# MLP up projection computed transposed: weights stationary, both parts of the activations moving

## The chip, the cores and the metric

The kernel runs on one core of a Trainium2 chip. The metric is the device time of one execution in microseconds (us). The engines of the core run side by side, each through its own list of instructions, and wait for one another on semaphores: TensorE (PE, matrix products; PEld is its loading of the held operand), VectorE (DVE), ScalarE (ACT), GpSimd (POOL) and SyncE (SP), which issues the loads from memory.

## What is computed

One call runs three transformer layers on 256 tokens of width 1024, in float32: an attention layer, an mLSTM layer and a hybrid layer. Each ends in the same MLP, and that is what the change touches:

```python
D_MODEL, SEQ, D_FF = 1024, 256, 4096
def sqrelu_mlp(h, w1, w2):
    return jnp.square(jax.nn.relu(h @ w1)) @ w2
# first_block, for both layers:
h = h + mix
h = h + sqrelu_mlp(rmsnorm(h, mlp_norm[layer]), mlp_w1[layer], mlp_w2[layer])
# hybrid_layer:
x = x + jnp.square(jax.nn.relu(rms_norm(x, norm_mlp) @ w_up)) @ w_down
gate = jax.nn.sigmoid(rms_norm(x, norm_ple) @ w_ple_gate)
x = x + gate * (p_l @ w_ple)
```

## The kernel before

**Products in three parts.** TensorE multiplies in the type fp32r. To keep float32 accuracy every operand is split in two: `hi`, its rounding to fp32r (a copy by ScalarE), and `lo`, the rest (a subtraction by VectorE). A product is three matmuls into the same sum: hi by hi, hi by the weights' lo, lo by the weights' hi. The helper `product` issues them:

```python
pe.matmul(o, hi, whi, start=start, stop=False)              # L693
pe.matmul(o, hi, wlo, start=False, stop=False)              # L694
return pe.matmul(o, lo, whi, start=False, stop=stop)        # L695
```

The second argument of `pe.matmul` is the operand that is held (loaded into the array first, 128 x 128), the third is the one that moves through, here 512 columns. So 128 tokens' activations are held and 512 weight columns move; the result has tokens on its partitions. The profile and the lists of instructions name a matmul by `result<-moving,held`.

**Weights.** A unit is 1024 columns of weights on 128 partitions (512 KB). SyncE loads units in the order in which they are used into a ring of eight places `raw`; ScalarE makes `w_hi` of a unit (L1199), VectorE `w_lo` (L1633), each into a ring of eight. TensorE adds one to the semaphore `unit_used` with the last matmul on a unit, which frees the three places: SyncE loads the unit that is eight further into it. `lo_ready` tells TensorE that a unit is split.

**The MLP.** The 4096 hidden columns are done in eight steps of 512 (`steps`, `HALF`). Step i has two halves. `up` multiplies the normalised activations `a_hi`, `a_lo` (eight chunks of 128 rows, all 256 tokens) by four units of w1, into the two banks of `pair[0]`. ScalarE takes relu of a bank (L1263), VectorE multiplies relu by the positive part of the same bank (L1679), which gives `hid`, tokens on partitions. For the second product `hid` must be held with hidden columns on partitions, so `turn_hidden` (L822 to L827) turns it by eight TensorE transposes of 128 x 128 into `turn_ps`; ScalarE copies that to `h_hi` (L1270), VectorE subtracts to get `h_lo` (L1688). `down_step` multiplies them by four units of w2 and adds into `down`, that is `pair[1]` and `score`, four banks that stay open over all eight steps (opened by four matmuls with zeros, L865).

**Order.** On TensorE: `up_first`, zeros, `turn_hidden`, then a hardware loop of seven rounds (L867): `up` of step i, `down_step` of step i-1, `turn_hidden` of step i; then `down_last` of step 7 (L829), which goes through the result in two halves, so that the additions to `x` and the turns of the next stage start early. `up_first` finishes the first 128 tokens of its last two units before the others and says so by `up_half`. ScalarE and VectorE run their own loops (L1280, L1698): `step` empties the `up` result, splits four units, and splits the turned `hid`; `step_tail` splits four more.

**Entry.** The activations of an MLP come from `x` through transposes into the two banks of `turn_ps` (`x_turn`, helper line L721), two chunks at a time; ScalarE and VectorE split each into `a_hi`, `a_lo` (L1214, L1651). Chunks 0 to 3 are turned in the stage before, chunks 4 to 7 after the first unit of `up_first` (its slot 0), as soon as VectorE has added the second half of the stage before to `x` (L1730). In the third MLP slot 3 turns `p_sb` too (group `pT.0`, its parts `p_hi`, `p_lo` at L1212 and L1649), an input of the stage behind it. A group of turns waits until the group two before it, in the same bank, has been read.

## Time and profile before

| | |
|---|---|
| median of 3 runs | 1225.9 us (1225.36 to 1228.71) |
| profiled execution, span | 1225.7 us |
| TensorE matmul busy | 1189.9 us, 97% |
| TensorE loads busy | 973.1 us, 79% |
| VectorE busy | 717.6 us, 59% |
| ScalarE busy | 618.9 us, 50% |
| DMA queue of SyncE | 52% of 16 engines, 199.61 MB |

Busy time of TensorE says little by itself: a matmul's record is longer than the distance to the next one's start, since they overlap. What a piece of work costs is read from the starts in the timeline. The line in a row is that of a helper, so work is told apart by the names of its tiles. The granted clock (PEclk) is a share of TensorE's full 2.4 GHz: 1.00 is that, 0.50 is 1.2 GHz. A row of the timeline gives the start, the length, the engine, the line, and in square brackets the idle time before it with what ended it.

### The profile page before, as it was taken

What the parts mean: (1) busy time and instruction counts of PE and PEld (TensorE: products, weight loads), DVE (VectorE), ACT (ScalarE), POOL (GpSimd) and SP (SyncE); (2) the same over time, 40 slices, a digit from 0 to 9 for tenths busy, and PEclk for the clock granted to TensorE, in tenths of its full rate; (3) what the DMA queues carried; (4) which work ended last, traced back from release to release, by engine and by line L of the source; (5) the groups of instructions that cost most, each with busy time, mean ns of one, the idle gap of its engine ahead of it and who ended that gap; (6) DMA issues with size and microseconds to landing.
All of it is one profiled execution on the core that took longest, in us unless ns stands there. A gap on an engine that the chain in (4) does not pass through costs nothing.

```text
span 1225.7 us, 15495 instructions
## 1 busy us (share of the span) xinstructions
PE 1189.9 (97%) x5530; PEld 973.1 (79%) x5530; DVE 717.6 (59%) x955; ACT 618.9 (50%) x970; POOL 63.4 (5%) x77
## 2 busy tenths in 40 slices
PE   6899999999999999999998999998999999999997
PEld 5778788888788888888887887767888887888876
DVE  4678655455566664554577778543645565554554
ACT  5487534434447653444356455465654444443443
POOL 2001000000000100000021033000000000000000
PEclk9999999999989999999999999999999999999999
DMA  8743555555445455555556555432565655555542
GB/s 245 257 131 116 166 172 188 188 175 186 144 129 162 150 179 185 186 185 184 176 161 195 161 172 167 125 103 70 171 189 174 189 180 171 186 188 182 180 150 90
DMA packets 95121, 205.58 MB, mean 168 GB/s; under 512 B 7805, under 2 KB 10149, under 8 KB 95072
## 3 DMA queue, kind: packets, MB, share of 16 engines
q1 hardware_dynamic: 93216, 199.61, 52.0%
q0 software_dynamic: 1696, 5.26, 1.6%
q8 instruction: 29, 0.48, 0.2%
q14 instruction: 20, 0.16, 0.0%
q10 hardware_dynamic: 160, 0.07, 0.0%
HBM read 203.86 MB, written 2.63 MB: 168 GB/s over the span
## 4 chain that ended last, share of the span: by engine, by line
PE 90%; DMA 4%; ACT 2%; DVE 2%; issue 1%; SPq 0%; POOL 0%; ACTq 0%
PE pair L693 24%; PE pair L695 23%; PE pair L694 23%; PE score L694 4%; PE score L693 4%; PE score L695 4%; PE turn_ps L721 3%; PE turn_ps L826 2%; DMA raw<-in_attn_w_in 1%; DMA bias<-bias_replicas 1%; DMA bias_replicas<-bias_scratch 1%; PE score L1077 1%; DVE w_lo L1633 1%; DMA raw<-in_w_in 0%; ACT w_hi L1199 0%
## 5 line engine op out<-in xcount | busy, mean ns | idle before, releaser
L1633 DVE TENSOR_TENSOR w_lo<-raw,w_hi 128x1024 fp32r<-128x1024 f32 (+2 forms) x381 | 453.4, 1223 | 157.4 <-ACT w_hi L1199 142.6
L1199 ACT ACTIVATE w_hi<-raw 128x1024 fp32r<-128x1024 f32 (+2 forms) x381 | 383.7, 1049 | 137.9 <-DMA raw<-in_w_in 31.4
L693 PE MATMUL pair<-w_hi,a_hi 128*128 128x512 f32 (+3 forms) x944 | 380.4, 403 | 4.5 <-ACT lat_sb L1244 3.4
L695 PE MATMUL pair<-w_hi,a_lo 128*128 128x512 f32 (+3 forms) x944 | 369.4, 391 | 0.0
L694 PE MATMUL pair<-w_lo,a_hi 128*128 128x512 f32 (+3 forms) x944 | 368.5, 390 | 0.0
L693 PEld LDWEIGHTS pair<-w_hi,a_hi 128*128 128x128 f32 x944 | 181.3, 192 | 42.3 <-ACT lat_sb L1244 3.6
L695 PEld LDWEIGHTS pair<-w_hi,a_lo 128*128 128x128 f32 x944 | 181.0, 192 | 37.4
L694 PEld LDWEIGHTS pair<-w_lo,a_hi 128*128 128x128 f32 x944 | 181.7, 192 | 34.7 <-issue 1.2
L1679 DVE SCALAR_TENSOR_TENSOR hid<-pair,relu 128x512 f32<-128x512 f32 x48 | 31.2, 686 | 116.2 <-ACT relu L1263 116.2
L1263 ACT ACTIVATE relu<-pair 128x512 f32<-128x512 f32 x48 | 26.4, 595 | 142.8 <-PE pair L695 142.8
L1688 DVE TENSOR_TENSOR h_lo<-turn_ps,h_hi 128x512 fp32r<-128x512 f32 x48 | 30.9, 685 | 112.6 <-ACT h_hi L1270 112.6
L1270 ACT ACTIVATE h_hi<-turn_ps 128x512 fp32r<-128x512 f32 x48 | 26.0, 595 | 137.1 <-PE turn_ps L826 137.1
L693 PE MATMUL pair<-w_hi,h_hi 128*128 128x512 f32 x192 | 75.5, 393 | 3.2 <-DVE h_lo L1688 3.2
L694 PE MATMUL pair<-w_lo,h_hi 128*128 128x512 f32 x192 | 75.6, 394 | 0.0
L694 PE MATMUL score<-w_lo,h_hi 128*128 128x512 f32 x192 | 75.6, 394 | 0.0
L693 PE MATMUL score<-w_hi,h_hi 128*128 128x512 f32 x192 | 75.5, 393 | 0.0
L695 PE MATMUL score<-w_hi,h_lo 128*128 128x512 f32 x192 | 74.7, 389 | 0.0
L695 PE MATMUL pair<-w_hi,h_lo 128*128 128x512 f32 x192 | 74.6, 388 | 0.0
L693 PEld LDWEIGHTS pair<-w_hi,h_hi 128*128 128x128 f32 x192 | 36.0, 188 | 12.0 <-issue 3.8
L693 PEld LDWEIGHTS score<-w_hi,h_hi 128*128 128x128 f32 x192 | 36.0, 188 | 8.3
L695 PEld LDWEIGHTS score<-w_hi,h_lo 128*128 128x128 f32 x192 | 36.0, 188 | 8.1
L695 PEld LDWEIGHTS pair<-w_hi,h_lo 128*128 128x128 f32 x192 | 36.0, 188 | 8.0
(335 smaller groups left out, 1225.4 us busy)
## 6 DMA issues: line engine op xcount, KB each, us to landing
raw<-in_mlp_w SPq DMA_DIRECT2D x128, 512.0 KB, 3.4
raw<-in_w_in SPq DMA_DIRECT2D x64, 512.0 KB, 3.7
raw<-in_w_up SPq DMA_DIRECT2D x32, 512.0 KB, 3.6
raw<-in_w_down SPq DMA_DIRECT2D x32, 512.0 KB, 3.2
raw<-in_attn_w_in SPq DMA_DIRECT2D x24, 512.0 KB, 7.1
raw<-in_mlstm_w_in SPq DMA_DIRECT2D x24, 512.0 KB, 3.8
raw<-in_w_br SPq DMA_DIRECT2D x16, 512.0 KB, 3.7
raw<-in_attn_w_out SPq DMA_DIRECT2D x8, 512.0 KB, 3.7
```

The costliest lines, as they stand in the source:

```text
L693: pe.matmul(o, hi, whi, start=start, stop=False)
L694: pe.matmul(o, hi, wlo, start=False, stop=False)
L695: return pe.matmul(o, lo, whi, start=False, stop=stop)
L721: last = pe.transpose(bank[:, j * P:(j + 1) * P], src, ident)
L826: last = pe.transpose(turn_ps[:, tt, c * P:(c + 1) * P], hid[:, tt, c * P:(c + 1) * P], ident)
L1077: last = pe.matmul(o, lq_t[rows, h // 2, q], lk_t[rows, h // 2, k], start=False, stop=True)
L1199: act.activation(w_hi[:, k % RING, 0:n], raw[:, k % RING, 0:n], ACT.Copy).then_inc(hi_ready, 1)
L1263: act.activation(relu[:, tt, :], pair[0][:, tt, :], ACT.Relu).then_inc(up_relu, 1)
L1270: act.activation(h_hi[:, :, tt * P:(tt + 1) * P], turn_ps[:, tt, :].rearrange("p (c s) -> p c s", s=P), ACT.Copy)\
L1633: dve.tensor_tensor(w_lo[:, k % RING, 0:n], raw[:, k % RING, 0:n], w_hi[:, k % RING, 0:n], ALU.subtract).then_inc(lo_ready, 1)
L1679: dve.scalar_tensor_tensor(hid[:, tt, :], pair[0][:, tt, :], 0.0, relu[:, tt, :], ALU.max, ALU.mult).then_inc(hid_ready, 1)
L1688: dve.tensor_tensor(h_lo[:, :, rows], turn_ps[:, tt, :].rearrange("p (c s) -> p c s", s=P), h_hi[:, :, rows], ALU.subtract).then_inc(hid_l ...
```

## The change

`up` holds the weights now and moves the activations, so that its result has hidden columns on partitions: what `turn_hidden` made. `a_hi` and `a_lo` become the two halves of one tile `a_both`, 512 columns for a chunk. With 128 columns of `w_hi` held, one matmul moves both (512 columns: hi sum in the first 256 columns of a bank, the lo by w_hi product in the others); with `w_lo` held, a second moves `a_hi` (256 columns) onto the second half. The four groups of 128 hidden columns have a bank each, two in `pair[0]` and two in `turn_ps` (together `ups`). ScalarE copies the second halves out (`up_low`), VectorE adds them to the first (`up_sum`) and multiplies by the positive part (`hid`). `h_hi`, `h_lo` come from `hid` in SBUF. The last step writes them to tiles of its own, `e_hi`, `e_lo`. `turn_hidden`, `relu` and the semaphores `up_relu`, `hid_turned` are gone; `up_copied`, `up_summed` are new. `up_first` does `pair[0]` for all four units, then `turn_ps` for all four; all four units are freed in the second pass. The turn of `p_sb` moves to slot 1, its splits before `step`, and the second pass waits for them. In the loops ScalarE and VectorE split six units before `h_hi`, `h_lo` and two after.

```diff
-        a_hi = sb("a_hi", [DC, S], F32R)
-        a_lo = sb("a_lo", [DC, S], F32R)
+        a_both = sb("a_both", [DC, 2, S], F32R)
+        a_hi, a_lo = (a_both[:, :, i, :] for i in range(2))
...
+        ups = [pair[0], turn_ps]
...
-                def up(k, it):
+                def up_unit(k, u, pairs):
+                    slot = (k + u) % RING
+                    for j in range(2):
+                        c = 2 * u + j
+                        for i in pairs:
+                            for b in range(2):
+                                at_col = j * HALF + (2 * i + b) * P
+                                cols = slice(at_col, at_col + P)
+                                pe.matmul(ups[i][:, b, :], w_hi[:, slot, cols], a_both[:, c, :, :],
+                                          start=c == 0, stop=False)
+                                last = pe.matmul(ups[i][:, b, S:], w_lo[:, slot, cols], a_hi[:, c, :],
+                                                 start=False, stop=c == DC - 1)
+                    return last
+
+                def up(k, h, it):
                     for u in range(4):
                         pe.wait_ge(lo_ready, at(k + u + 1, it, RING))
-                        for tt in range(TT):
-                            for j in range(2):
...
+                        if u == 0:
+                            pe.wait_ge(up_summed, at(h, it, 2))
+                        up_unit(k, u, range(2)).then_inc(unit_used, 1)
...
                 def up_first(k):
...
+                    for u in range(4):
                         wait_source(source, 2 * u + 1)
                         pe.wait_ge(lo_ready, k + u + 1)
-                        products(u, 0)
-                        products(u, 1).then_inc(unit_used, 1)
+                        last = up_unit(k, u, [0])
+                        if u == 3:
+                            last.then_inc(up_half, 1)
                         if u in slots:
                             slots[u]()
...
+                    if last_split:
+                        pe.wait_ge(turn_dve, turn[last_split]["dve_end"])
+                    for u in range(4):
+                        up_unit(k, u, [1]).then_inc(unit_used, 1)
...
-                            if n == 0:
-                                pe.wait_ge(hid_lo, h + tt + 1)
...
-                                last = product(down[n][:, tt, :], h_hi[:, u, rows], h_lo[:, u, rows],
+                                if n == 0 and tt == 0 and u % 2 == 0:
+                                    pe.wait_ge(hid_lo, h + u // 2 + 1)
+                                last = product(down[n][:, tt, :], e_hi[:, u, rows], e_lo[:, u, rows],
...
-                turn_hidden(h0)
                 with pe.Fori(1, steps) as i:
-                    up(k0 - 4, i)
+                    up(k0 - 4, h0, i)
                     down_step(k0, h0 - TT, i)
-                    turn_hidden(h0, i)
...
-            mlp(2, "x6", {0: lambda: (x_turn(6, 4), x_turn(6, 6)), 3: p_turn},
-                lambda: (x_turn(7, 0), x_turn(7, 2)))
+            mlp(2, "x6", {0: lambda: (x_turn(6, 4), x_turn(6, 6)), 1: p_turn},
+                lambda: (x_turn(7, 0), x_turn(7, 2)), "pT.0")
...
-                        act.activation(relu[:, tt, :], pair[0][:, tt, :], ACT.Relu).then_inc(up_relu, 1)
...
+                        act.activation(up_low[:, 2 * i:2 * i + 2, :], ups[i][:, :, S:], ACT.Copy).then_inc(up_copied, 1)
+                    for u in range(4 if it is None else 6):
                         split_unit(k + 8 + u, it)
...
+                    if it is not None:
+                        act.wait_ge(unit_used, at(k + 8, it, RING))
+                    for i in range(2):
+                        act.wait_ge(hid_ready, at(h + i + 1, it, TT))
+                        act.activation(hi[:, 2 * i:2 * i + 2, :], hid[:, 2 * i:2 * i + 2, :], ACT.Copy)\
                             .then_inc(hid_hi, 1)
...
                 split_until(k0 + 7)
+                if meanwhile:
+                    meanwhile()
...
-                        dve.scalar_tensor_tensor(hid[:, tt, :], pair[0][:, tt, :], 0.0, relu[:, tt, :],
...
+                    for i in range(2):
+                        dve.wait_ge(up_copied, at(h + i + 1, it, TT))
+                        dve.tensor_tensor(up_sum[:, 2 * i:2 * i + 2, :], ups[i][:, :, 0:S],
+                                          up_low[:, 2 * i:2 * i + 2, :], ALU.add)\
+                            .then_inc(up_summed, 1)
```

TensorE, where a round of the first MLP's loop ends and `down_last` begins. Before, with the last product of `down_step`, the transposes, and the first product of `down_last`:

```order
L693 MATMUL score<-w_hi,h_hi 128x512
L694 MATMUL score<-w_lo,h_hi 128x512
L695 MATMUL score<-w_hi,h_lo 128x512
L824 REGISTER_ALU
L826 MATMUL turn_ps<-square,hid 128x128 [waits hid_ready]
L826 MATMUL turn_ps<-square,hid 128x128 x3
L824 REGISTER_ALU
L826 MATMUL turn_ps<-square,hid 128x128 [waits hid_ready]
L826 MATMUL turn_ps<-square,hid 128x128 x3
L867 REGISTER_ALU
L867 COMPARE_AND_BRANCH
L693 MATMUL pair<-w_hi,h_hi 128x512 [waits hid_lo,lo_ready]
```

Now:

```order
L697 MATMUL score<-w_hi,h_hi 128x512
L698 MATMUL score<-w_lo,h_hi 128x512
L699 MATMUL score<-w_hi,h_lo 128x512
L859 REGISTER_ALU
L859 COMPARE_AND_BRANCH
L697 MATMUL pair<-w_hi,e_hi 128x512 [waits hid_lo,lo_ready]
```

The eight transposes are gone, and the wait of `down_last` is for a split that does not come from them.

TensorE, the entry of the first MLP's loop with the first products of `up`. Before, then now:

```order
L865 MATMUL score<-zeros 128x512 x2
L826 MATMUL turn_ps<-square,hid 128x128 [waits hid_ready]
L826 MATMUL turn_ps<-square,hid 128x128 x3
L826 MATMUL turn_ps<-square,hid 128x128 [waits hid_ready]
L826 MATMUL turn_ps<-square,hid 128x128 x3
L867 UNCONDITIONAL_BRANCH
L867 ISA
L693 MATMUL pair<-w_hi,a_hi 128x512 [waits lo_ready]
L694 MATMUL pair<-w_lo,a_hi 128x512
L695 MATMUL pair<-w_hi,a_lo 128x512
```

```order
L858 MATMUL score<-zeros 128x512 x2
L859 UNCONDITIONAL_BRANCH
L859 ISA
L804 REGISTER_ALU [waits lo_ready]
L794 MATMUL pair<-a_both,w_hi 128x512 [waits up_summed]
L796 MATMUL pair<-a_both,w_lo 128x256
```

The wait for `hid` before the transposes is now one for the sums before `up`, and three matmuls of one shape have become two of two shapes.

VectorE at the entry of the third MLP, behind the splits of the activations. Before, then now (`raw`, `w_hi`, `w_lo`: two weight units; `p_lo`: the split of the turned `p_sb`):

```order
L1633 TENSOR_TENSOR w_lo<-raw,w_hi 128x1024 [waits hi_ready] x2
L1679 SCALAR_TENSOR_TENSOR hid<-pair,relu 128x512 [waits up_relu]
L1649 TENSOR_TENSOR p_lo<-turn_ps,p_hi 128x256 [waits turn_act]
L1649 TENSOR_TENSOR p_lo<-turn_ps,p_hi 128x256
L1679 SCALAR_TENSOR_TENSOR hid<-pair,relu 128x512 [waits up_relu]
```

```order
L1625 TENSOR_TENSOR w_lo<-raw,w_hi 128x1024 [waits hi_ready] x2
L1641 TENSOR_TENSOR p_lo<-turn_ps,p_hi 128x256 [waits turn_act]
L1641 TENSOR_TENSOR p_lo<-turn_ps,p_hi 128x256
L1671 TENSOR_TENSOR up_sum<-pair,up_low 128x512 [waits up_copied]
L1671 TENSOR_TENSOR up_sum<-turn_ps,up_low 128x512 [waits up_copied]
L1677 SCALAR_TENSOR_TENSOR hid<-up_sum 128x512 [waits up_summed] x2
```

`p_lo` stands before all work on the `up` result, and behind the two weight splits.

## Rows read from the trace of the kernel before

**Rows 1.** Page, part 4: the chain that ended last, shares by line

```profile
PE pair L693 24%; PE pair L695 23%; PE pair L694 23%; PE score L694 4%; PE score L693 4%; PE score L695 4%; PE turn_ps L721 3%; PE turn_ps L826 2%; DMA raw<-in_attn_w_in 1%; DMA bias<-bias_replicas 1%; DMA bias_replicas<-bias_scratch 1%; PE score L1077 1%; DVE w_lo L1633 1%; DMA raw<-in_w_in 0%; ACT w_hi L1199 0%
```

**Rows 2.** Timeline of TensorE: end of loop round 1, start of round 2

```profile
173.64 1.03 PE L826 MATMUL turn_ps<-square,hid 128*128 128x128 f32 x8
174.43 0.47 PE L693 MATMUL pair<-w_hi,a_hi 128*128 128x512 f32 x1
174.74 0.39 PE L694 MATMUL pair<-w_lo,a_hi 128*128 128x512 f32 x1
```

**Rows 3.** Windows: round 2 (length, busy us by engine, clock, DMA); page part 6: weight loads

```profile
174.43:197.20 22.77, 22.77 (x107) 18.84 (x106) 11.84 (x12) 9.73 (x13) 0.00 (x0) 1.00 0.57 184
...
raw<-in_mlp_w SPq DMA_DIRECT2D x128, 512.0 KB, 3.4
```

**Rows 4.** Windows: first MLP's last transposes to `down_last`; timeline: its first matmul

```profile
310.36:312.46 2.10, 1.03 (x9) 0.82 (x8) 0.83 (x2) 1.46 (x3) 0.00 (x0) 1.00 0.52 109
...
312.46 0.47 PE L693 MATMUL pair<-w_hi,h_hi 128*128 128x512 f32 x1 [1.07 <-DVE h_lo L1688]
```

**Rows 5.** Timelines of TensorE and its loads: first and last starts of even runs

```profile
177.28 0.39 PE L693 MATMUL pair<-w_hi,a_hi 128*128 128x512 f32 x1
...
185.21 0.39 PE L695 MATMUL pair<-w_hi,a_lo 128*128 128x512 f32 x1
...
335.91 0.19 PEld L693 LDWEIGHTS pair<-w_hi,a_hi 128*128 128x128 f32 x1
...
336.81 0.23 PEld L695 LDWEIGHTS pair<-w_hi,a_lo 128*128 128x128 f32 x1
...
632.45 0.31 PE L694 MATMUL pair<-w_lo,a_hi 128*128 128x320 f32 x1
...
635.81 0.34 PE L693 MATMUL pair<-w_hi,a_hi 128*128 128x384 f32 x1
...
940.39 0.40 PE L693 MATMUL pair<-w_hi,b_hi 128*128 128x512 f32 x1
...
950.15 0.40 PE L693 MATMUL pair<-w_hi,b_hi 128*128 128x512 f32 x1
```

**Rows 6.** Timelines of TensorE and VectorE: entry of the first MLP

```profile
137.87 0.39 PE L693 MATMUL pair<-w_hi,a_hi 128*128 128x512 f32 x1
...
138.56 1.28 DVE L1730 TENSOR_TENSOR x<-x,pair 128x512 f32<-128x512 f32 x2
...
140.61 1.03 PE L721 MATMUL turn_ps<-square,x 128*128 128x128 f32 x8
...
142.12 1.66 DVE L1651 SCALAR_TENSOR_TENSOR a_lo<-turn_ps,gains,a_hi 128x256 fp32r<-128x256 f32 x4 [2.28 <-ACT a_hi L1214]
...
149.66 0.61 PE L865 MATMUL pair<-zeros 128*128 128x512 bf16 x2
...
150.49 0.69 DVE L1679 SCALAR_TENSOR_TENSOR hid<-pair,relu 128x512 f32<-128x512 f32 x1 [1.51 <-ACT relu L1263]
...
151.64 0.47 PE L693 MATMUL pair<-w_hi,a_hi 128*128 128x512 f32 x1
```

**Rows 7.** Timelines of TensorE and VectorE: entry of the third MLP

```profile
1003.20 0.39 PE L693 MATMUL pair<-w_hi,a_hi 128*128 128x512 f32 x1
...
1005.93 1.04 PE L721 MATMUL turn_ps<-square,x 128*128 128x128 f32 x8
...
1011.34 2.36 DVE L1633 TENSOR_TENSOR w_lo<-raw,w_hi 128x1024 fp32r<-128x1024 f32 x2 [2.24 <-ACT w_hi L1199]
...
1016.32 0.75 DVE L1649 TENSOR_TENSOR p_lo<-turn_ps,p_hi 128x256 fp32r<-128x256 f32 x2 [2.01 <-ACT p_hi L1212]
...
1018.13 0.47 PE L693 MATMUL pair<-w_hi,a_hi 128*128 128x512 f32 x1
```

**Rows 8.** Windows near the program's start: an idle stretch and the clock after

```profile
22.00:24.50 2.50, 0.36 (x2) 0.00 (x0) 2.46 (x4) 2.47 (x5) 0.00 (x0) 1.00 1.05 320
26.00:30.00 4.00, 4.00 (x13) 3.10 (x12) 3.13 (x7) 1.42 (x4) 0.95 (x2) 0.57 0.34 121
```

## What will it do to the time? The prediction, made before the run

> **What bounds the kernel now.** First the chain of work that ended last, by line [rows 1]: about three quarters of the span is matmuls of the one helper that multiplies (L693 to L695), and `PE turn_ps L826`, the transposes of `hid`, is 2%. So time is won or lost where TensorE's instructions start later or earlier. Next the timeline of TensorE around one MLP step [rows 2]: a matmul of 512 columns starts about 0.23 us after the one before, although its own duration reads 0.39 us (matmuls overlap). So I count by distances between starts, not by durations. The eight transposes start at 173.64 and the first up matmul at 174.43, 0.79 us; the second up matmul comes 0.31 us after the first instead of 0.23 us. A set of transposes in mid-loop thus costs 0.79 + 0.08 = 0.87 us. The stretch of a whole step [rows 3] is 22.77 us, with no idle time on TensorE, VectorE busy 11.84 us and ScalarE 9.73 us: inside the loops TensorE alone sets the pace. The three MLPs do 8 steps each; 7 of the 8 `up`s of each lie in a loop.
>
> **The transposes between steps go.** In each MLP `turn_hidden` runs before the loop, six times between two steps, and once before `down_last`. The six cost 0.87 us each [rows 2]: 3 x 6 x 0.87 = 15.7 us gained.
>
> **The last set goes with its wait.** After the last loop step TensorE transposes, then waits for ScalarE and VectorE to split the result: from 310.36 to 312.46, 2.10 us, 1.07 of it idle [rows 4], and again the slow second matmul, 0.08. Now the split (`e_hi`, `e_lo`) needs only the sums, which are there about 2 us after `up` ends, and the last `down_step` (some 11 us) lies between. Nothing is late next: the weights of `down_last` are split in that same time, as now. 3 x 2.18 = 6.5 us gained.
>
> **The up products themselves.** Before: 48 matmuls of 512 columns and 48 weight loads. After: 32 matmuls of 512 columns (`w_hi` held, both parts of the activations moving), 32 of 256 (`w_lo` held), 64 weight loads; the columns are the same, 24576. No row has this form at 256 columns, so I bound it. The rows give starts at full clock [rows 5]: 35 intervals from 177.28 to 185.21, 0.2266 us at 512 columns; 23 intervals from 632.45 to 635.81, 0.1461 us at 320. The slope is 0.419 ns a column, so 256 columns come to 0.1193 us. A pair (512 and 256) is 0.3459 us against 1.5 x 0.2266 = 0.3399 us: 6.0 ns more, x 32 = 0.19 us an `up`. For the 21 ups in loops 4.0 us lost; the three first ones are counted below. The lower bound is the weight load: with 8 columns eight loads run from 335.91 to 336.81, 0.1125 us each [rows 5]; a pair is then 0.3391 us and the 21 ups gain 0.5 us. The upper bound: where the held operand lies elsewhere (`b_hi`, `b_lo`) 42 intervals from 940.39 to 950.15 give 0.2324 us at 512 columns [rows 5]. Place matters by up to 5.8 ns, for a reason that the trace does not show, and here other tensors are held. With 5.8 ns on each matmul the 21 ups lose 11.8 us. I take the line through the two `a_hi` rows, the nearest in form.
>
> The Trainium skill's page "TensorE: Matmul & The Clock Gate", section "Back-to-back issue gap", gives N/2.4 + 2.5 ns warm, 216 and 109 ns. By it a pair would cost as much as 1.5 old matmuls (325 against 324 ns) and the 4.0 us would vanish; the rows stand about 10 ns above it at 512 columns, so the rows decide, and this sum is not used.
>
> **VectorE and ScalarE in the loop.** ScalarE swaps two Relu for two copies. VectorE gets two adds more, taken as 0.65 us each after its `hid` operation [rows 6]: 11.84 + 1.3 = 13.1 us of 22. No cost while that cover stands. Two new waits: `up` of the next step needs both sums (about 1.5 us after the last up matmul, with 11 us of `down_step` between), and ScalarE's `h_hi` must wait until `down_step` has read the old one; queued behind that on ScalarE are two weight splits, and TensorE wants `h_lo` only after a whole `up`. Four operations, some 2.5 us, against 10.9 us. ScalarE now splits six units ahead of it; the sixth slot is freed half way through `down_step` and a load lands 3.4 us after issue [rows 3], in time. Cost 0; if it broke, all 21 steps would pay.
>
> **The start of an MLP gets worse.** `up_first` now does half its columns for all four units, then the other half. (1) The turns of the last four chunks of x are issued after 4 pairs, 1.38 us, instead of 2.74 us. In the first MLP [rows 6] it starts at 137.87, so they are reached at 139.25; but VectorE's two additions to `x` start at 138.56 and take 1.28: 139.84, 1.97 us after the start. Turns at 139.88. (2) With 0.87 for the turns the second unit begins at 140.75 and ends at 142.13. Its successor needs two `a_lo`; these start 1.51 us after the turns (140.61, 142.12) and take 0.83: 142.28. (3) Two more half units end at 145.05, the second pass (16 pairs, 5.53) at 150.58, against 149.66 before: 0.92 later. (4) Before, `hid` ended at 151.18, 1.52 us after the last up matmul's turn; the next `up` began at 151.64, in effect 151.72 with the slow second matmul. Now it waits for the add, which I take as long as the `hid` operation (0.69): 150.58 + 1.56 = 152.14. Lost: 0.42 us, in the first and second MLP.
>
> In the third [rows 7] the second pass writes the bank in which `pT.0` is turned, so TensorE waits for `p_lo`; queued before that on VectorE are two `w_lo`, behind ScalarE's squares and splits. Start 1003.20; `x` ready 1.97 us later as in the first, seen by TensorE at 1005.20, so the turns come 0.73 us sooner than before (1005.93) and the splits behind them too. The `w_lo` pair starts at 1011.34 and ends 2.28 later, less 0.73: 1012.89; `p_lo` takes 0.75, so TensorE goes on at 1013.65. The first pass, with the 0.48 us of p turns and a short wait for their bank, is done at 1010.85: 2.8 us idle. Then 5.53 + 1.56: the next `up` at 1020.74 against 1018.13 + 0.08. Lost: 2.5 us. All three starts: 0.42 + 0.42 + 2.5 = 3.4 us (rounded up).
>
> **The clock after that wait.** Near the start of the program TensorE is busy for 0.36 of 2.5 us, and the four microseconds from 26 on run at a granted clock of 0.57, most of them at the lower level of 1.2 GHz [rows 8]; after an idle time of 1.07 us the clock stayed at 1.00 [rows 4]. A stop of 2.8 us is on the far side of both, so I count the same stretch again, 4 x 0.43 = 1.7 us lost.
>
> **Sum.** 15.7 + 6.5 - 4.0 - 3.4 - 1.7 = 13.1 us. From the span of 1225.7 us: 1212.6; the median of the runs is 0.2 us above the span, so 1212.8 us.
>
> **Rivals.** *The clock stays full* in the third MLP: 1211.1 us; within the forecast's own range.
>
> *The added weight loads are not hidden* (slower). 16 loads more in each of 24 ups, each at the 0.1125 us at which loads follow each other [rows 5]: 24 x 16 x 0.1125 = 43.2 us instead of the 4.0 (and the little in the starts), so about 1252 us. It decides from 17.1 us of cost, that is 45 ns for each added load, or 22 ns a pair. Against it: at 320 columns matmuls start every 0.146 us while one load reads 0.19 us, so load and matmul overlap there. Same page of the Trainium skill, "What overlaps and what doesn't": weight loads overlap matmuls only in other row groups. By that rule this rival holds; the trace speaks against it.
>
> *The held operands' place costs the upper bound*: 7.8 us more than forecast, 1220.6 us. For: three rates are seen in one kernel. Also, `a_hi` and `a_lo` are interleaved now, which could move the rate of all other stages that hold them, either way.
>
> *A new wait in the loop*: `h_hi` late because ScalarE sits on the sixth unit's load. One us a step would be 21 us and about 1234 us, slower; 8 us of slack speak against it.
>
> *It does not do what it says*: the order of instructions has no transpose of `hid` left; excluded.
>
> **Chances.** Forecast with either clock 0.70; upper bound of the held operands 0.13; faster than forecast (pair at its lower bound, 1208) 0.06; loads not hidden 0.05; new wait 0.03; something that eats the gain to nothing 0.03. Range 1207.5 to 1221 takes in both bounds of the pair and both clocks. About 0.3% can be told from no change: 3.7 us. Faster 0.89, same 0.03, slower 0.08.
>
> **What would show it.** In the changed kernel: starts of up pairs 0.346 us apart; a step of 22.77 - 0.87 + 0.19 = 22.1 us with no idle; `down_last` starting 0.23 us after the last `down_step` matmul; 0.6 us idle at each MLP's start and 2.8 in the third, with a clock below 1 behind it. Wrong would be: a pair over 0.362 us, idle time on TensorE inside a loop, or stages outside the MLPs at a new rate.

## The result

| | kernel before | changed kernel |
|---|---|---|
| median, measured side by side | 1227.3 us (1225.4 to 1232.2, 4 runs) | 1210.5 us (1209.9 to 1211.2, 4 runs) |
| profiled execution, span | 1225.7 us | 1208.1 us |
| ratio, 95% interval | | 0.988 (0.985 to 0.991) |

The forecast was 1212.8 us, the forecast's range 1207.5 to 1221.0. The time lies 2.3 us below the forecast and inside the range. That closeness is partly luck, as the traces show: the MLPs gave 11.0 us, and 6.5 us came from stretches that the change doesn't touch.

The page of the changed kernel, parts 1 and 4 (busy time, share and count of each engine; shares of the chain that ended last), to be read beside [rows 1]:

```profile
PE 1170.8 (97%) x5722; PEld 965.5 (80%) x5722; DVE 748.1 (62%) x1003; ACT 628.5 (52%) x970; POOL 63.5 (5%) x77
...
PE pair L697 16%; PE pair L699 16%; PE pair L698 16%; PE turn_ps L794 7%; PE pair L794 7%; PE turn_ps L796 4%; PE score L699 4%; PE score L697 4%; PE score L698 4%; PE pair L796 4%; PE turn_ps L725 3%; DMA raw<-in_w_in 1%; DVE w_lo L1625 1%; DMA raw<-in_attn_w_in 1%; SPq L644 1%
```

The transposes of `hid` are gone from the chain. L794 (`w_hi` held, 512 columns) and L796 (`w_lo` held, 256) have taken the place of a quarter of the old products. VectorE is busy 30 us longer than before, ScalarE 10 us.

Timeline of TensorE: pairs of `up` in the second pass of `up_first`; the end of the last `down_step` and the start of `down_last`; the windows of loop rounds of the first MLP (length, busy us of PE, PEld, DVE, ACT and POOL, granted clock, DMA):

```profile
143.22 0.39 PE L794 MATMUL turn_ps<-a_both,w_hi 128*128 128x512 f32 x1
143.45 0.27 PE L796 MATMUL turn_ps<-a_both,w_lo 128*128 128x256 f32 x1
143.56 0.40 PE L794 MATMUL turn_ps<-a_both,w_hi 128*128 128x512 f32 x1
...
304.27 0.39 PE L699 MATMUL score<-w_hi,h_lo 128*128 128x512 f32 x1
304.50 0.39 PE L697 MATMUL pair<-w_hi,e_hi 128*128 128x512 f32 x1
...
171.37:182.46 11.09, 11.09 (x65) 9.77 (x64) 4.27 (x5) 3.17 (x4) 0.00 (x0) 1.00 0.55 179
193.45:204.74 11.29, 11.29 (x65) 9.80 (x64) 4.21 (x5) 3.16 (x4) 0.00 (x0) 1.00 0.56 188
...
171.37:193.45 22.08, 22.08 (x113) 18.79 (x112) 13.20 (x15) 10.16 (x12) 0.00 (x0) 1.00 0.56 188
193.45:215.75 22.30, 22.30 (x114) 18.82 (x113) 13.12 (x15) 10.16 (x12) 0.00 (x0) 1.00 0.56 190
```

The last `down_step` runs into `down_last` without a stop (0.23 us from start to start, where [rows 4] had 2.10 us and a wait). The windows are two `up`s that follow each other in the loop (11.09 and 11.29 us), and then their whole rounds: 22.08 and 22.30 us instead of the 22.77 of [rows 3], TensorE never idle, VectorE busy 13.1 to 13.2. That two equal rounds differ by 0.2 us comes back below.

Timeline of TensorE at the start of the first MLP (the square brackets: idle time before, and what ended it), to be read beside [rows 6]:

```profile
134.43 0.39 PE L794 MATMUL pair<-a_both,w_hi 128*128 128x512 f32 x1
...
136.45 1.09 PE L725 MATMUL turn_ps<-square,x 128*128 128x128 f32 x8 [0.47 <-DVE x L1728]
...
141.83 0.39 PE L794 MATMUL turn_ps<-a_both,w_hi 128*128 128x512 f32 x1
...
147.38 0.61 PE L858 MATMUL pair<-zeros 128*128 128x512 bf16 x2
...
148.96 0.50 PE L794 MATMUL pair<-a_both,w_hi 128*128 128x512 f32 x1 [0.53 <-DVE up_sum L1671]
```

The same of the third MLP, with VectorE's two rows that end TensorE's wait, and windows of the stop and of what comes behind it, to be read beside [rows 7]:

```profile
988.08 0.39 PE L794 MATMUL pair<-a_both,w_hi 128*128 128x512 f32 x1
...
993.20 0.66 PE L725 MATMUL turn_ps<-square,p_sb 128*128 128x128 f32 x4 [0.62 <-DMA p_sb<-in_p]
...
995.54 2.36 DVE L1625 TENSOR_TENSOR w_lo<-raw,w_hi 128x1024 fp32r<-128x1024 f32 x2 [2.24 <-ACT w_hi L1190]
997.82 0.75 DVE L1641 TENSOR_TENSOR p_lo<-turn_ps,p_hi 128x256 fp32r<-128x256 f32 x2
...
998.63 0.50 PE L794 MATMUL turn_ps<-a_both,w_hi 128*128 128x512 f32 x1 [1.99 <-DVE p_lo L1641]
...
997.00:999.00 2.00, 0.37 (x2) 0.34 (x3) 2.00 (x4) 0.48 (x1) 0.00 (x0) 1.00 0.00 0
999.00:1001.00 2.00, 2.00 (x13) 1.78 (x12) 0.17 (x1) 0.00 (x0) 0.00 (x0) 1.00 0.00 0
```

The wait for `p_lo` is there, in the place and the order that was forecast (two `w_lo`, then `p_lo`, then TensorE), but it is 1.99 us and not 2.8. Behind it the clock reads 1.00, the full 2.4 GHz.

**Where the 17.6 us between the two traces come from.** I cut both traces at the same events. "Entry" runs from the first `up` matmul of an MLP to the first `up` matmul in the loop, "rest" from there to the start of the last `down_last` matmul (all in us):

| | before | changed | difference |
|---|---|---|---|
| start of program to first MLP | 137.87 | 134.43 | -3.44 |
| entries of the three MLPs | 13.77, 13.80, 14.93 | 14.53, 14.56, 17.77 | +0.76, +0.76, +2.84 |
| rest of the three MLPs | 172.55, 172.48, 172.49 | 167.19, 167.73, 167.20 | -5.36, -4.75, -5.29 |
| first to second MLP | 116.55 | 113.14 | -3.41 |
| second to third MLP | 376.18 | 376.50 | +0.32 |
| behind the third MLP | 28.56 | 28.56 | 0.00 |

The MLPs give 11.0 us. The other 6.5 us stand in stages whose work is the same in both kernels. So there are two questions: is the change to be thanked for the 6.5 us, and which of my terms were off?

### The profile page after: what moved, and what is told of

Its sections match the earlier page's. It is cut to its first block, busy times and chain, and to the rows that moved or that the text cites. A ratio compares the mean times of both kernels' runs of the same rounds, so it can differ in the third digit from the quotient of the medians.

```text
span 1208.1 us, 15885 instructions
## 1 busy us (share of the span) xinstructions
PE 1170.8 (97%) x5722; PEld 965.5 (80%) x5722; DVE 748.1 (62%) x1003; ACT 628.5 (52%) x970; POOL 63.5 (5%) x77
## 4 chain that ended last, share of the span: by engine, by line
PE 89%; DVE 3%; DMA 3%; ACT 3%; SPq 1%; issue 1%; POOL 0%; ACTq 0%
PE pair L697 16%; PE pair L699 16%; PE pair L698 16%; PE turn_ps L794 7%; PE pair L794 7%; PE turn_ps L796 4%; PE score L699 4%; PE score L697 4%; PE score L698 4%; PE pair L796 4%; PE turn_ps L725 3%; DMA raw<-in_w_in 1%; DVE w_lo L1625 1%; DMA raw<-in_attn_w_in 1%; SPq L644 1%
## 5 line engine op out<-in xcount | busy, mean ns | idle before, releaser
L697 PE MATMUL pair<-w_hi,a_both 128*128 128x512 f32 (+3 forms) x560 | 226.1, 404 | 5.1 <-ACT lat_sb L1235 4.1
L699 PE MATMUL pair<-w_hi,a_both 128*128 128x512 f32 (+3 forms) x560 | 217.1, 388 | 0.0
L698 PE MATMUL pair<-w_lo,a_both 128*128 128x512 f32 (+3 forms) x560 | 216.5, 387 | 0.0
L794 PE MATMUL pair<-a_both,w_hi 128*128 128x512 f32 x384 | 143.5, 398 | 1.6 <-DVE up_sum L1671 1.6
L794 PE MATMUL turn_ps<-a_both,w_hi 128*128 128x512 f32 x384 | 142.6, 396 | 2.0 <-DVE p_lo L1641 2.0
L697 PEld LDWEIGHTS pair<-w_hi,a_both 128*128 128x128 f32 x560 | 107.1, 191 | 28.8 <-ACT lat_sb L1235 4.4
L699 PEld LDWEIGHTS pair<-w_hi,a_both 128*128 128x128 f32 x560 | 106.7, 191 | 21.8
L698 PEld LDWEIGHTS pair<-w_lo,a_both 128*128 128x128 f32 x560 | 107.3, 192 | 19.9 <-issue 1.2
L796 PE MATMUL pair<-a_both,w_lo 128*128 128x256 f32 x384 | 107.6, 280 | 0.0
L796 PE MATMUL turn_ps<-a_both,w_lo 128*128 128x256 f32 x384 | 107.5, 280 | 0.0
L794 PEld LDWEIGHTS pair<-a_both,w_hi 128*128 128x128 f32 x384 | 72.1, 188 | 20.5 <-DVE up_sum L1671 3.1
L794 PEld LDWEIGHTS turn_ps<-a_both,w_hi 128*128 128x128 f32 x384 | 72.0, 188 | 19.5 <-DVE p_lo L1641 2.3
L796 PEld LDWEIGHTS pair<-a_both,w_lo 128*128 128x128 f32 x384 | 72.5, 189 | 0.9
L796 PEld LDWEIGHTS turn_ps<-a_both,w_lo 128*128 128x128 f32 x384 | 72.5, 189 | 0.0
```

What stands on the lines that cost most here:

```text
L794: pe.matmul(ups[i][:, b, :], w_hi[:, slot, cols], a_both[:, c, :, :], start=c == 0, stop=False)
L796: last = pe.matmul(ups[i][:, b, S:], w_lo[:, slot, cols], a_hi[:, c, :], start=False, stop=c == DC - 1)
```

## The experiments

In all of them the MLPs are compared by the same cuts, since two executions of one kernel differ outside the MLPs by as much as an effect in them. Unless said otherwise, an edit is made to the changed kernel.

### Both kernels again

No edit.

> The kernel before, unchanged, profiled a second time. Two stages outside the MLPs were shorter in the changed kernel's trace: the time up to the first MLP (134.4 against 137.9 us) and the stretch between the first two MLPs (113.1 against 116.6 us). Theory A (chance of an execution: the loads behind the attention bias, and when the clock falls in the narrow gate matmuls): this trace gives other values for the two than the first did, by a microsecond or more, while each MLP stays at 186.3, 186.3 and 187.4 us within 0.3. Theory B (the change does it, by the place of a_both): 137.9 and 116.6 again within 0.5 us.

> The changed kernel, profiled and timed again. Theory A (the gain proper is the MLPs' 11.0 us, the rest chance): MLPs at 181.7, 182.3 and 185.0 us within 0.3 each, but the time up to the first MLP and between the first two moves by a microsecond or more; the clock stays full behind the 2.0 us stop in the third MLP. Theory B: all stretches as in the first trace within 0.5 us. Time 1210 to 1215 us by A, 1210.5 by B.

Measured: spans 1221.3 and 1211.3 us; the changed kernel's median 1214.0 us (1209.2 to 1216.4, 4 runs) against 1226.0 us (1222.2 to 1233.2, 13 runs), ratio 0.990 (0.984 to 0.995). MLPs of the kernel before: 186.25, 186.25, 187.38; of the changed one: 181.71, 181.89, 184.86. That is 11.4 us, beside 11.0 in the first pair of traces. The second MLP of the changed kernel is 0.4 us below its first trace, more than the 0.3 that was expected. Start of program to first MLP: 134.81 before, 136.80 changed, the other way round than in the first pair (137.87 and 134.43). First to second MLP: 114.67 and 114.77, no difference.

So the 6.5 us are chance of an execution and not the change. The traces of the changed kernel and of all its relatives below, twelve in all, say the same: the first MLP starts between 133.98 and 138.20 us, and from the first to the second are 113.10 to 116.57 us. Windows of two places where the first pair of traces parts, in the kernel before and then in the changed kernel:

```profile
54.87:58.78 3.91, 0.00 (x1) 0.00 (x0) 3.88 (x5) 1.48 (x2) 0.00 (x0) 0.77 0.48 148
...
337.00:347.00 10.00, 10.00 (x38) 9.13 (x39) 3.68 (x9) 3.14 (x7) 0.00 (x0) 0.50 0.29 88
```

```profile
52.31:53.81 1.50, 0.00 (x1) 0.03 (x1) 1.34 (x2) 1.50 (x4) 0.00 (x0) 1.00 0.57 169
...
331.50:334.80 3.30, 3.30 (x11) 2.72 (x11) 1.78 (x5) 2.58 (x5) 0.00 (x0) 0.50 0.48 124
335.00:345.00 10.00, 10.00 (x45) 7.66 (x44) 5.24 (x16) 4.52 (x6) 0.00 (x0) 1.00 0.54 143
```

TensorE waits 3.91 us in the first attention layer for its bias in one trace and 1.50 us in the other. Behind the first MLP the clock is at half for more than ten microseconds in one and for some three in the other. In the second trace of the kernel before the first of these stops is 1.23 us: the long one does not belong to that kernel.

### The up products in the old form

```diff
-  pe.matmul(ups[i][:, b, :], w_hi[:, slot, cols], a_both[:, c, :, :], ...)
-  last = pe.matmul(ups[i][:, b, S:], w_lo[:, slot, cols], a_hi[:, c, :], ...)
+  last = product(ups[i][:, j, :], a_hi[:, c, rows], a_lo[:, c, rows],
+                 w_hi[:, slot, cols], w_lo[:, slot, cols], u == 0, u == 3)
```

> The changed kernel with the up products in the old form: activations held, 512 weight columns moving, 48 matmuls an up instead of 64, spread over the same four banks. The rest is as in the changed kernel, so what comes out of the up products is in the wrong layout and summed over half the chunks in each bank; the output is not the reference's, only the time counts. Theory 1 (the new form costs 0.3498 us for what took 0.3399): 32 x 9.9 ns less in each of 24 ups, 7.6 us less than the changed kernel, and a loop round of 21.9 us instead of 22.2. Theory 2 (the new form costs nothing, the 3.8 us that the MLPs fell short are waits): within 1 us of the changed kernel, round 22.2 us. Theory 3 (waits in the loop): the round is the same and idle time stands in it.

Measured: 1206.6 us (1206.0 to 1209.3), ratio 0.984 (0.979 to 0.988). The rest of an MLP is 164.85 us in all three, against 167.19, 167.73 and 167.20 in the changed kernel. Together that is 7.6 us for 21 `up`s in loops, 11 ns a pair, where the sum had 4.0 and 6.0: theory 1 holds. Timeline of TensorE in this kernel, first and last of eight starts:

```profile
179.79 0.39 PE L699 MATMUL turn_ps<-w_hi,a_both 128*128 128x512 f32 x1
...
181.38 0.39 PE L697 MATMUL turn_ps<-w_hi,a_both 128*128 128x512 f32 x1
```

Seven intervals in 1.59 us are 0.227 us each, the old rate of [rows 5]; an `up` is 10.88 us in every round but the first (11.09 or 11.29 in the changed kernel) and a round 21.87. The tensors and the banks here are those of the changed kernel, with `a_hi` and `a_lo` interleaved in `a_both`. So neither the new place of the activations nor the banks in `turn_ps` make the pair dearer. What is left is the form itself, and this run changes several things of it at once: which operand is held, and so from which tensor it is loaded, which one moves, and the mixture of sizes with its loads. The place of the held operand is not excluded: the old form holds `a_hi` and `a_lo`, the new one `w_hi` and `w_lo`. Nor has the old form one rate for all tensors: a `down_step` has it too, 48 matmuls of 512 columns with `h_hi` or `h_lo` held, and takes 10.98 to 11.01 us, 0.229 us each and not 0.227.

This run also gives the other side of the sum. Nothing but the transposes and the wait of the last set is taken away in its rest: 172.5 - 164.85 = 7.65 us an MLP, 23.0 in all, where I had 15.7 + 6.5 = 22.2. A set in mid-loop is worth 22.77 - 21.87 = 0.90 us (forecast 0.87), the last one with its wait 7.65 - 6 x 0.90 = 2.25 (2.18).

### Three matmuls of 256 columns

```diff
-  pe.matmul(ups[i][:, b, :], w_hi[:, slot, cols], a_both[:, c, :, :], start=c == 0, stop=False)
+  pe.matmul(ups[i][:, b, 0:S], w_hi[:, slot, cols], a_hi[:, c, :], start=c == 0, stop=False)
+  pe.matmul(ups[i][:, b, S:], w_hi[:, slot, cols], a_lo[:, c, :], start=False, stop=False)
```

> The changed kernel, but the matmul of 512 columns with w_hi held is cut in two of 256, each with its own load of w_hi: 96 matmuls and 96 loads an up, same columns and same sums. In the changed kernel a start after a 512 column matmul comes 233 ns later, after a 256 column one 116.5. Theory 1 (each matmul with its own load costs its streaming time and a fixed 14.8 ns): 3 x 121.5 = 364.5 ns instead of 349.6, 32 x 14.9 ns an up, 11.4 us more over 24 ups. Theory 2 (a matmul of 256 columns starts its successor after 116.5 ns, whatever it is): 349.5 ns, no change. Theory 3 (loads are the bound at 256 columns, 0.1115 us each): 334.5 ns, 11.6 us less. Rival of the prediction (a load is not hidden under 256 columns): over 0.45 us, 75 us more.

Measured: 1220.4 us (1219.3 to 1223.0, 10 runs), ratio 0.996 (0.994 to 0.998). The rest of an MLP is 169.26 us, 2.07 more than in the changed kernel. The three whole MLPs are 184.07, 184.10 and 187.24 us, 6.4 more in all: theory 1 had 11.4 and theory 2 nothing, so the cost lies between them, somewhat nearer to theory 1. Its timeline, first and last of fourteen starts:

```profile
196.42 0.28 PE L794 MATMUL turn_ps<-a_both,w_hi 128*128 128x256 f32 x1
196.54 0.28 PE L796 MATMUL turn_ps<-a_both,w_hi 128*128 128x256 f32 x1
...
197.98 0.28 PE L796 MATMUL turn_ps<-a_both,w_hi 128*128 128x256 f32 x1
```

Thirteen intervals in 1.56 us: 0.120 us at 256 columns, each with a load of its own. The line through 320 and 512 columns had 0.1193. So that part of my working holds in this form too: with `w_hi` or `w_lo` held, a matmul of 256 columns is within 1 ns of it, and no 5.8 ns are added. A load and a matmul more for the same columns in each of the 32 products of an `up` cost 2.07 us / (7 x 32) = 9 ns, far from the 45 ns from which the rival with loads that are not hidden decides, or the 112.5 ns that it charged.

### Another order of the same matmuls

In the changed kernel and its relatives the `up` of a loop round has one of two lengths: 11.10 (or 11.09) and 11.29 (or 11.30) us, that is 0.3467 and 0.3529 us a pair. The first of each MLP's seven is left out here and below; it starts behind a stop or the zeros and is in most traces 0.1 to 0.2 us longer. In some MLPs they come in turn, in others all rounds take the longer one; the second MLP of the changed kernel has only the longer, in its second execution the two in turn. The `down_step`s, 10.98 to 11.01 us, don't do it. Three orders were tried. The first is made on the changed kernel, the other two, like the one that repeats the first, on the kernel with both mends (see the end of this part), whose MLPs are 180.68, 180.72 and 181.53 us. All matmuls of 512 columns of a chunk first:

```diff
-for i in pairs:
-    for b in range(2):
-        (512 columns with w_hi held, then 256 with w_lo held)
+for part in range(2):
+    for i in pairs:
+        for b in range(2):
+            (part 0: 512 columns with w_hi held; part 1: 256 with w_lo held)
```

> The changed kernel, but in each chunk of up the four matmuls of 512 columns (w_hi held) come first, then the four of 256 (w_lo held), instead of alternating. Loads, columns and sums are the same; output as before. In the changed kernel alternating matmuls start 0.233 us after a start of 512 columns and 0.1165 after one of 256, 0.3498 a pair, while even runs give 0.2266 at 512 (kernel before) and 0.120 at 256 (the run with three matmuls of 256). Theory A, the change of size costs: 3 x 0.2266 + 0.233 + 3 x 0.120 + 0.1165 = 1.389 us for four pairs, 0.3473 a pair, so 2.5 ns x 32 = 0.08 us less an up and 0.6 us less an MLP, 1.8 us in all. Theory B, the moving of a_both costs 0.233 whatever stands beside it: 4 x 0.233 + 4 x 0.120 = 1.412 us, 0.353 a pair, 0.1 us more an up, 0.8 us more an MLP, 2.4 us in all slower. To be read from the starts and from the lengths of the MLPs (the changed kernel: 181.7 and 184.9), since the median of a run moves by more than that.

Groups of two (`for i`, `for part`, `for b`):

```diff
 for i in pairs:
-    for b in range(2):
-        (512 columns, then 256)
+    for part in range(2):
+        for b in range(2):
+            (part 0: 512 columns; part 1: 256)
```

> The kernel with both mends, with the matmuls of an up in groups of two: two of 512 columns, then two of 256. In the traces so far the up of a loop round takes one of exactly two lengths where the sizes alternate, 11.10 or 11.29 us (0.3467 or 0.3529 us a pair), in some MLPs turn by turn, in others always the longer one; with groups of four it is 11.21 to 11.23 us (0.3506 a pair) in every round, in the old form 10.88. Theory A, the two lengths belong to the strict alternation of sizes: groups of two give a single length in all rounds, near 11.2 us, MLPs of about 180.8. Theory B, they are two courses that TensorE falls into whatever the order, the one by chance of how an up begins: two lengths here too, MLPs from 180.3 (the shorter one always) to 181.8 (the longer one always).

The banks in another order, sizes alternating:

```diff
-for i in pairs:
-    for b in range(2):
+for b in range(2):
+    for i in pairs:
```

> The kernel with both mends, sizes alternating as in it, but the four groups of 128 hidden columns in another order, so that successive pairs write banks of pair and turn_ps in turn. Output as before. Theory A, the longer and the shorter up come from which bank is written when (two pairs into one tensor, then two into the other): one length here, or two others than 11.10 and 11.29 us. Theory B, the banks have nothing to do with it: 11.10 and 11.29 us again, in turn or always the longer one; MLPs 180.7 to 181.8, some 1206 us.

Measured:

| | median, us | ratio (95%) | `up`s in the loops, us | MLPs, us |
|---|---|---|---|---|
| groups of four | 1212.2 (1210.2 to 1212.8, 6 runs) | 0.989 (0.987 to 0.992) | all 11.22 or 11.23 | 181.83, 181.83, 185.07 |
| groups of two | 1207.5 (1205.6 to 1211.7, 4 runs) | 0.987 (0.983 to 0.991) | all 11.14 to 11.16 | 180.63, 180.62, 181.00 |
| other banks | 1208.1 (1206.6 to 1211.1, 4 runs) | 0.987 (0.983 to 0.991) | 11.10 and 11.29 in turn | 180.86, 180.88, 181.27 |

Timeline of TensorE with groups of four; a row stands for two matmuls (x2):

```profile
180.40 0.63 PE L796 MATMUL pair<-a_both,w_hi 128*128 128x512 f32 x2
180.87 0.62 PE L796 MATMUL turn_ps<-a_both,w_hi 128*128 128x512 f32 x2
181.33 0.40 PE L799 MATMUL pair<-a_both,w_lo 128*128 128x256 f32 x2
181.56 0.40 PE L799 MATMUL turn_ps<-a_both,w_lo 128*128 128x256 f32 x2
181.80 0.63 PE L796 MATMUL pair<-a_both,w_hi 128*128 128x512 f32 x2
```

Four matmuls of 512 columns take 0.93 us, 0.2325 each, three of the four behind one of their own size; four of 256 take 0.47, 0.1175 each, to within 0.0025 since the rows have steps of 0.01. Over the other six rounds of the first MLP the mean distances are 0.232 and 0.118. Neither theory's sum came out: four pairs take 1.40 us and not 1.389 or 1.412. The change of size is not what makes the large one dearer (theory A), and the small one is a little below its 0.120 (theory B). The matmuls of 512 columns with weights held are on average dearer than 0.227 in every order.

The other two settle what the two lengths are. With groups of two there is one length only, as with groups of four, so the two lengths belong to the strict alternation of sizes. With other banks both are there, to the hundredth, so it is not this order of the banks that makes them. Which one a round falls into is not settled: TensorE is never idle in either kind, and VectorE, ScalarE and the DMA are equally busy in both (the four windows of the changed kernel above). Grouping in twos is the shortest inside the MLPs, by 0.7 us over three of them, in one trace of each order; a median doesn't show so little, and two traces of the changed kernel differ by 0.5 us in the same sum.

### The last step shares `h_hi` and `h_lo`

```diff
-  last = product(down[n][:, tt, :], e_hi[:, u, rows], e_lo[:, u, rows], ...)
+  last = product(down[n][:, tt, :], h_hi[:, u, rows], h_lo[:, u, rows], ...)
...
-  if it is not None:
+  if it is not None or k != k0:
       act.wait_ge(unit_used, at(k + 8, it, RING))
...
-                step(k0 + 4 + RING * (steps - 2), h0 + TT * (steps - 1), hi=e_hi, lo=e_lo)
+                step(k0 + 4 + RING * (steps - 2), h0 + TT * (steps - 1))
```

> The changed kernel, but the last step's split goes into the tiles h_hi and h_lo that the last down_step still reads, as in the loop, so it must wait for that step's end. Theory: of the 2.18 us that I put on the last set of transposes with its wait, 0.87 are transposes and the rest is the wait for the split, which two tiles more remove. Then TensorE stands idle before down_last for ScalarE's copy and VectorE's subtraction, 0.2 + 0.6 + 0.7 = 1.5 us, less what its last matmul covers: each MLP 1.3 to 1.5 us longer (183.1, 183.2, 186.4 us), 4.2 us in all. Rival: the split of the last step is not on the path (its sums are ready 11 us earlier): no change. The time from start to end moves by two or three microseconds between executions, so the MLPs' lengths decide.

Measured: 1219.0 us (1215.0 to 1221.0, 10 runs), ratio 0.994 (0.992 to 0.997). Timelines of TensorE and ScalarE where `down_last` begins:

```profile
306.34 0.40 PE L699 MATMUL score<-w_hi,h_lo 128*128 128x512 f32 x1
...
308.27 0.47 PE L697 MATMUL pair<-w_hi,h_hi 128*128 128x512 f32 x1 [1.54 <-DVE h_lo L1684]
...
306.77 1.15 ACT L1261 ACTIVATE h_hi<-hid 128x512 fp32r<-128x512 f32 x2 [6.12 <-PE score L699]
```

From 306.34 to 308.27 are 1.93 us where 0.23 would be an ordinary distance, and the second matmul comes 0.08 late again: 1.8 us in each MLP, 5.3 in all, somewhat over the 4.2 that were expected. The MLPs are 184.20, 183.61 and 187.42 us, 1.3 to 2.5 more than in the changed kernel, the rest of the spread being the long and short `up`s. Of the 6.75 us that the last sets gave (3 x 2.25) 5.3 thus hang on `e_hi` and `e_lo` alone, nearly a quarter of the 23.0 us of both kinds of transposes. Without them the split has to wait for the last `down_step`, as ScalarE's row shows, and TensorE for the split.

### The turns of `p_sb` moved behind `up`

```diff
-                    if last_split:
-                        pe.wait_ge(turn_dve, turn[last_split]["dve_end"])
...
+                            if n == 0 and tt == 0 and mid_slot:
+                                mid_slot()
...
-            mlp(2, "x6", {0: lambda: (x_turn(6, 4), x_turn(6, 6)), 1: p_turn},
-                lambda: (x_turn(7, 0), x_turn(7, 2)), "pT.0")
+            mlp(2, "x6", {0: lambda: (x_turn(6, 4), x_turn(6, 6))},
+                lambda: (x_turn(7, 0), x_turn(7, 2)), p_turn)
...
-            mlp(2, lambda: split_turn("pT.0"))
...
+            mlp(2)
...
+            split_until(groups["pl0"]["units"][0][0] + 2)
+            split_turn("pT.0")
...
```

> The changed kernel, but p_sb is turned in down_last, after its first quarter, and split there by ScalarE and VectorE between the weight units of the next stage, instead of at the entry of the third MLP. Theory: the third entry's 2.0 us stop and the 0.6 us wait for the load of p_sb are the price of turning it early; the third MLP then takes what the first does plus 0.56 us for the four transposes, 182.3 instead of 184.9 us, and the stage behind it does not change (28.6 us to the last matmul). Rival 1: VectorE's additions to x start late because p_lo stands before them, and the stage behind the MLP grows by a microsecond. Rival 2: the third entry waits for something else next (the weights' splits): it stays above 14.5 us.

Measured: 1209.2 us (1206.8 to 1215.9, 4 runs), ratio 0.986 (0.981 to 0.991). The entry of the third MLP is 14.67 us instead of 17.77, like that of the other two. The whole third MLP is 182.32 us, 2.5 to 2.7 us less than in the two traces of the changed kernel. The stretch behind it, where the turns now stand, is 28.60 against 28.56: nothing is given back. The price of the wait on `p_lo` is shown, and that it buys nothing.

### A longer stop in the same place

```diff
                     if last_split:
                         pe.wait_ge(turn_dve, turn[last_split]["dve_end"])
+                        pe.wait_ge(up_summed, h0 + 1)
```

> The changed kernel, but the second pass of up_first waits for the sum of the first too, which VectorE makes right behind p_lo in the third MLP. The stop there grows from 2.0 to 2.7 us; in the others the sum is not ready either when the second pass starts, so they wait some 2 us as well. Theory 1 (a stop of 2.7 us, as I had forecast, lowers the granted clock): the clock goes below 1 behind it in the third MLP, which takes 185.6 + 1.7 = 187.3 us. Theory 2 (it takes a longer one): the clock stays at 1.00 and the third MLP takes 185.6 us.

Measured: 1215.0 us (1212.7 to 1218.2, 6 runs), ratio 0.992 (0.989 to 0.996). In the third MLP TensorE stops for 2.50 us. Timeline, and windows of the stop and behind it:

```profile
1001.67 0.47 PE L794 MATMUL turn_ps<-a_both,w_hi 128*128 128x512 f32 x1 [2.50 <-DVE up_sum L1672]
...
999.17:1001.67 2.50, 0.00 (x0) 0.03 (x1) 2.35 (x4) 0.68 (x2) 0.00 (x0) 1.00 0.00 0
1001.67:1003.00 1.33, 1.33 (x7) 1.18 (x8) 0.00 (x0) 0.00 (x0) 0.00 (x0) 1.00 0.00 0
1003.00:1005.00 2.00, 2.00 (x13) 1.76 (x12) 0.00 (x0) 0.00 (x0) 0.00 (x0) 1.00 0.28 55
```

The clock stays at 1.00: in this execution a stop of nearly the forecast length did not cost the 1.7 us. The third MLP takes 186.19 us, of which some 0.5 are `up`s that all take the longer length; theory 2 had 185.6 and theory 1 187.3. That a longer stop would do it, as theory 2 adds, is not shown, and the last section has stops that speak against the length alone. The first two MLPs are 182.39 and 182.25 us. They were expected to wait too and don't: the added wait stands inside `if last_split`, so in the third alone. The stop was meant to be 2.7 us and came out at 2.50; whether 2.8 us there would have brought the clock down is not shown.

### Both mends, and with the grouping too

The first kernel has the turns of `p_sb` behind `up`, as above. It also lets `up` begin with `pair[0]` as soon as the first sum is there, and waits for the second before it writes `turn_ps`:

```diff
 if u == 0:
-    pe.wait_ge(up_summed, at(h, it, 2))
-up_unit(k, u, range(2)).then_inc(unit_used, 1)
+    pe.wait_ge(up_summed, at(h - 1, it, 2))
+    up_unit(k, u, [0])
+    pe.wait_ge(up_summed, at(h, it, 2))
+    up_unit(k, u, [1]).then_inc(unit_used, 1)
+else:
+    up_unit(k, u, range(2)).then_inc(unit_used, 1)
```

> As the one before, and the first up of a loop round waits only for the first sum before it writes the two banks of pair, and for the second before it writes the other two. Theory: the 0.5 us of idle time between the zeros and the first up of each MLP goes; from the zeros to that up 0.95 us instead of 1.57. MLPs at 181.1, 181.1 and 181.7 us; against the changed kernel 2.6 + 3 x 0.6 = 4.4 us less. Rival: ScalarE empties both banks late, and the wait moves to the second pair of banks: as the kernel before it.

> The kernel with both mends (the turns of the third MLP's p moved behind up, and the second half of an up's wait split off), with the same grouping by size as the run before. MLPs of the kernel with both mends: 180.68, 180.72, 181.53. Theory A: 180.1, 180.1, 180.9, some 1203.8 us against 1205.6. Theory B: 181.5, 181.5, 182.3, some 1208 us.

Measured, first kernel: 1205.6 us (1204.0 to 1207.1, 6 runs), ratio 0.984 (0.980 to 0.987). Entries 13.65, 13.66, 13.79 us: 0.9 us less than in the changed kernel in two MLPs, 4.0 in the third. MLPs 180.68, 180.72, 181.53: 6.0 us less than in the changed kernel, where 4.4 were expected, and 17.1 less than before. Timeline of the same place as 147.38 to 148.96 above:

```profile
147.38 0.59 PE L862 MATMUL score<-zeros 128*128 128x512 bf16 x2
147.63 0.58 PE L794 MATMUL pair<-a_both,w_hi 128*128 128x512 f32 x1
```

No idle time stands between the zeros and `up`. With the groups of four as well (second kernel): 1208.6 us (1206.0 to 1211.6, 6 runs), ratio 0.987 (0.984 to 0.989), MLPs 180.85, 180.86, 181.32. Summed that is 543.0 us beside 542.9, so the 3 us between the medians come from outside the MLPs, and this grouping does nothing here either. By the lengths of the MLPs the kernel with both mends beats the two that this case began with; its median is below theirs too, though its interval (0.980 to 0.987) touches that of the changed kernel (0.985 to 0.991).

## Why the forecast came out near, step by step

| term of the sum | forecast, us | shown, us |
|---|---|---|
| transposes between steps, and the last set with its wait | +22.2 | +23.0 |
| up products in loops | -4.0 | -7.6 |
| starts of the MLPs | -3.4 | -4.4 |
| clock behind the stop | -1.7 | 0 |
| the three MLPs | +13.1 | +11.0 and +11.4 |
| stages that the change doesn't touch | 0 | +6.5 in one pair of traces, -1.4 in the other |

**What bounds the kernel: right.** VectorE went from 11.84 to 13.1 or 13.2 us a round, as worked out, and nothing came of it. Neither of the two new waits in the loop shows as idle time. The rounds are 22.08 and 22.30 us, or all 22.28, where 22.1 was forecast.

**The last set: right.** 0.23 us from the last `down_step` matmul to `down_last`, and the kernel that shares the tiles shows the wait that would else take its place.

**The up pairs: right in direction, the size wrong.** The forecast pair of 0.3459 us is the shorter of the two courses (0.3467) to 1 ns. The longer one (0.3529) is taken by half of the rounds or by all. The step that failed is "I take the line through the two `a_hi` rows, the nearest in form": it took the 0.2266 us of 512 columns over from another form, and it took one rate for all rounds. At 256 columns the line held (0.120 for 0.1193); at 512 the starts are 0.2325 us apart in groups of four, which is the 0.2324 of the upper bound's `b_hi` rows. Measured are 10.88 us for the old `up` and 11.10 or 11.29 for the new: 0.22 or 0.41 us more, where the sum had 0.19. With the changed kernel's mixture the 21 `up`s lost 7.6 us and not 4.0. The upper bound of 11.8 us held. Its reason, the place of the held operand, is neither shown nor excluded: it does not add 5.8 ns to every matmul, since those of 256 columns stand at 0.120 with `w_hi` and `w_lo` held, but at 512 columns no run holds the same tensor in both forms.

**The Trainium skill's two rules.** By the Trainium skill's page "TensorE: Matmul & The Clock Gate", section "Back-to-back issue gap" (216 and 109 ns), the changed pair would cost no more than the old product; the run with the old form shows some 11 ns less than the changed pair, and the groups of four stand at some 232 and 118 ns. That section of the Trainium skill gives the formula for isolated matmuls, and for a stream with loads some 131 ns at 512 columns. No row here comes near that. By the same page of the Trainium skill, "What overlaps and what doesn't", loads don't overlap matmuls of the same row group; here a load and a matmul more per product cost 9 ns, while one load's own record reads 0.19 us. So the measurements decide against both rules for this type and form. The text ahead of that list in the Trainium skill also lets a load into the background weight buffer go ahead of running matmuls. That would fit the 9 ns, though no row tells which buffer a load went to.

**The starts: right in kind.** In the first MLP the turns came 2.02 us after the start (forecast 2.01), the second pass took 5.55 (5.53), and `up` began 1.58 us behind it (1.56). Only the first pass took 7.40 instead of 7.18 us, through dearer pairs and a short wait in front of the third unit. And I credited the new entry with the 0.08 us by which the second matmul comes late in the old one, though it comes late in the new one too. So the entry is 0.76 us longer and not 0.42. (Step 2 of that sum also has a slip: 139.88 + 1.51 + 0.83 is 142.22 and not 142.28.) In the third MLP the second pass began 10.55 us after the start (forecast 10.45), so the chain of splits before `p_lo` was read rightly. The idle time before it was 1.99 us and not 2.8 because the first pass had taken longer; 0.62 us of that is a wait for the load of `p_sb`, which I had not seen: moving the turn from slot 3 to slot 1 moved it ahead of its data.

**The clock: wrong.** I took one case ([rows 8]) for what a stop of 2.8 us does anywhere. No stop in the third MLP, neither of 1.99 nor of 2.50 us, brought it below 1.00. The term was not open to a forecast from the length of the stop at all: one and the same stop of 3.17 us is followed by full clock in one trace of the changed kernel and by half in the other (last section).

**The untouched stages** can't be forecast: they differ by 3 us between executions of one kernel. The MLPs gave 11.0 and 11.4 us where the sum said 13.1, so it was some 2 us too high, although the medians (16.8 and 12.0 us apart) taken alone would have called it too low or just right.

The rivals: loads not hidden, a new wait in the loop and the full price of the held operand's place (11.44 us an `up`) are excluded by the `up`s of 11.1 and 11.3 us and the rounds without idle time. A part of that price, at 512 columns alone, is not. That `a_both`, being interleaved, moves the rate of the other stages is excluded by the stretch behind the third MLP, 28.56 us in both.

## What to carry to other kernels

Where two products follow each other and the result of the first has to be held for the second, let the first one's weights be held, so that the result comes out turned: a step of 22.8 us lost its transposes at the price of a few ns a matmul. Price each form of matmul by runs of starts of exactly that form (what is held, what moves, how many columns), since with columns and tensors equal the new form cost 7 to 13 ns on the 340 of a pair. Look at what a moved step waits for in its new place, at the loads that feed it too: one turn moved ahead of its data and its readers cost 2.5 us, and moving it behind the work gave them all back.

## What the hardware showed that I had not expected

- **The same columns at several rates.** On the same tensors and banks a matmul of 512 columns starts every 0.227 us with `a_hi` and `a_lo` held and every 0.2325 with `w_hi` held, in groups of four; with `h_hi` and `h_lo` held (`down_step`) it is 0.229, with `b_hi` and `b_lo` 0.2324 ([rows 5]). At 256 columns no such surcharge stands: 0.120 with the weights held. Whether the roles do it or the places of the operands is open.
- **The small one is a little cheaper in company.** 256 columns take 0.120 us in an even run and some 0.118 in groups of four between matmuls of 512. Also open.
- **Two courses of one loop.** With sizes alternating, an `up` is 11.10 or 11.29 us, in turn or always the longer, in one and the same program. Groups of two give 11.14 to 11.16. The difference between the two courses would be 4 us over 21 `up`s.
- **The clock and stops.** Behind 1.99 and 2.50 us of idle TensorE in the third MLP it stayed at 2.4 GHz. Near 22 us it stayed there behind 1.72 us (first fence: the kernel with the turns of `p_sb` moved) and was at 1.2 GHz behind 2.69 us (first three of the second fence: the one with both mends). The length of the stop alone does not decide. In the kernel before only 2.19 us of idle time (last row of the second fence) stood ahead of the 0.57 of [rows 8]. And both traces of the changed kernel have a stop of 3.17 us near 838 us, in the same work: the third fence has the stop and the clock behind it in the first trace, 1.00, the fourth those of the second trace, 0.50. What decides is not settled.

```profile
22.00:24.00 2.00, 0.46 (x3) 0.04 (x1) 2.00 (x4) 1.97 (x4) 0.00 (x0) 1.00 1.04 313
24.00:26.00 2.00, 1.82 (x7) 0.93 (x8) 0.30 (x2) 1.84 (x4) 0.91 (x2) 1.00 1.05 397
26.00:30.00 4.00, 4.00 (x19) 3.33 (x18) 3.25 (x7) 2.44 (x5) 0.60 (x1) 1.00 0.34 105
```

```profile
22.00:24.00 2.00, 0.00 (x0) 0.00 (x0) 1.87 (x3) 1.97 (x4) 0.00 (x0) 1.00 1.04 317
24.00:26.00 2.00, 1.85 (x4) 0.36 (x4) 0.44 (x1) 1.69 (x4) 0.91 (x2) 0.54 1.05 397
26.00:30.00 4.00, 4.00 (x10) 3.13 (x11) 3.10 (x7) 1.15 (x2) 0.60 (x1) 0.50 0.20 71
...
24.55 0.33 PE L721 MATMUL turn_ps<-square,gain_rows 128*128 128x128 f32 x1 [2.19 <-DMA square<-in_c_square]
```

```profile
838.10 0.55 PE L725 MATMUL turn_ps<-square,l_work 128*128 128x128 f32 x3 [3.17 <-ACT l_work L1494]
...
838.10:840.10 2.00, 2.00 (x10) 1.71 (x11) 0.15 (x1) 1.87 (x4) 0.00 (x0) 1.00 0.00 0
840.10:844.10 4.00, 4.00 (x22) 3.42 (x21) 1.59 (x2) 1.60 (x4) 0.00 (x0) 1.00 0.40 101
```

```profile
839.82 0.55 PE L725 MATMUL turn_ps<-square,l_work 128*128 128x128 f32 x3 [3.17 <-ACT l_work L1494]
...
841.00:844.30 3.30, 3.30 (x10) 2.56 (x9) 1.23 (x1) 0.84 (x1) 0.00 (x0) 0.50 0.02 5
```
